# Routing done tile by tile between the output projection's matmuls, in a transformer block with 32 experts

## The reference

```
x += concat[GLA heads, stick-breaking heads] @ w_out
x += cross_attention(rmsnorm(x), rmsnorm(mem))          # ends with o @ w_mo
h  = rmsnorm(x, g_ffn)
logits = h @ w_router + b_router                        # 512 x 32
top_vals, top_idx = top_k(logits, 4)
gates = softmax(top_vals)
# pairs (token, expert) sorted by expert, in blocks of rows of one expert
for each block (rows xb, expert e):
    gu = xb @ w_gu[e] + b_gu[e]                         # 1024 -> 2048
    gate = min(gu[:, :1024], 7);  lin = clip(gu[:, 1024:], -7, 7)
    act = (lin + 1) * gate * sigmoid(1.702 * gate)
    y = act @ w_down[e] + b_down[e]                     # 1024 -> 1024
    x[token] += gates * y
y = rmsnorm(x, g_final)
```

## Time and profile before

| | us |
|---|---|
| median of 3 runs | 1733.54 (1732.9 to 1734.62) |
| the profiled execution | 1732.56 |
| its span, first to last instruction | 1730.7 |
| mean granted TensorE clock in it, as a share of full speed | 0.977 |
| busy in the span: PE / DVE / ACT / POOL | 1643.1 / 1075.6 / 831.3 / 133.2 |
| weights and data moved | 477.05 MB, 276 GB/s on average |

### The profile page before, as it was taken

The page is one execution under the profiler, slowest core; times in us unless marked ns, Lnnn a source line. Parts: engine busy times, 40 slices in busy tenths (PEclk is TensorE's granted clock), DMA queues, the critical chain, the costliest instruction groups (busy, mean ns, idle before and its releaser), DMA issues.

```text
span 1730.7 us, 26767 instructions
## 1 busy us (share of the span) xinstructions
PE 1643.1 (95%) x9998; PEld 1370.3 (79%) x9998; DVE 1075.6 (62%) x1139; ACT 831.3 (48%) x844; POOL 133.2 (8%) x216
## 2 busy tenths in 40 slices
PE   6999989999975999999999999999999999999995
PEld 5876657987744888888888888888888888888883
DVE  4221554434346677777777777777777777777774
ACT  4243364433321454555545555555555555555553
POOL 0020220000000000100001000010000100000000
PEclk9999989999987999999999999999999999999998
DMA  5111123422066899999999999999999999999993
GB/s 203 49 49 49 49 98 122 143 73 93 25 227 218 278 366 366 377 368 368 370 367 382 364 370 368 368 384 357 373 373 361 387 357 374 369 372 369 369 356 116
DMA packets 134772, 477.05 MB, mean 276 GB/s; under 512 B 10241, under 2 KB 10290, under 8 KB 134706
## 3 DMA queue, kind: packets, MB, share of 16 engines
q1 hardware_dynamic: 123968, 446.72, 69.1%
q0 software_dynamic: 7168, 25.17, 6.1%
q10 hardware_dynamic: 3602, 4.69, 0.9%
HBM read 457.67 MB, written 18.87 MB: 275 GB/s over the span
## 4 chain that ended last, share of the span: by engine, by line
PE 91%; DVE 4%; ACT 3%; issue 1%; DMA 1%; ACTq 0%; POOL 0%; DVEq 0%; POOLq 0%
PE psum L978 23%; PE psum L997 21%; PE psum L1022 21%; PE psum L610 17%; PE psum L789 1%; PE psum L778 1%; PE psum L972 1%; PE psum L964 1%; PE psum L766 1%; PE psum L881 1%; PE psum L901 1%; ACT ring_split L1116 1%; PE psum L915 0%; DVE ring_split L1509 0%; PE psum L889 0%
## 5 line engine op out<-in xcount | busy, mean ns | idle before, releaser
L978 PEld LDWEIGHTS psum<-MIX,ring 128*128 128x128 f32 x4096 | 775.7, 191 | 101.6 <-DVE MIX L1923 1.6
L978 PE MATMUL psum<-MIX,ring 128*128 128x96 f32 x4096 | 726.0, 260 | 1.1 <-DVE MIX L1923 1.1
L997 PE MATMUL psum<-ring_split,xs_hi 128*96 128x512 f32 x512 | 200.3, 437 | 0.0
L1884 DVE TENSOR_TENSOR ring_split<-ring,w_hi_a 128x2048 fp32r<-128x2048 f32 x64 | 146.3, 2288 | 84.2 <-ACT w_hi_a L1366 83.9
L1022 PE MATMUL psum<-ring_split,act_hi 128*96 128x512 f32 x512 | 198.1, 434 | 0.0
L1896 DVE TENSOR_TENSOR ring_split<-ring,w_hi_x 128x2048 fp32r<-128x2048 f32 x62 | 141.9, 2288 | 84.8 <-ACT w_hi_x L1377 84.8
L1884 DVE TENSOR_TENSOR ring_split<-ring,w_hi_x 128x2048 fp32r<-128x2048 f32 x64 | 146.4, 2289 | 72.2 <-ACT w_hi_x L1366 72.2
L610 PE MATMUL psum<-ring_split,H_hi 128*128 128x512 f32 (+1 forms) x512 | 151.2, 379 | 0.6 <-DVE ring L1595 0.6
L1896 DVE TENSOR_TENSOR ring_split<-ring,w_hi_a 128x2048 fp32r<-128x2048 f32 x62 | 141.6, 2284 | 2.5 <-ACT w_hi_a L1377 2.5
L1366 ACT ACTIVATE w_hi_a<-ring 128x2048 fp32r<-128x2048 f32 x62 | 117.7, 1898 | 12.3 <-DMA ring<-in_w_gu 12.3
L1366 ACT ACTIVATE w_hi_x<-ring 128x2048 fp32r<-128x2048 f32 x64 | 121.3, 1897 | 0.0
(11 more groups left out here) (290 smaller groups left out, 2656.8 us busy)
## 6 DMA issues: line engine op xcount, KB each, us to landing
ring<-in_w_gu SPq DMA_DIRECT2D x256, 1024.0 KB, 10.6
ring<-in_w_down SPq DMA_DIRECT2D x128, 1024.0 KB, 12.7
ring<-in_w_in SPq DMA_DIRECT2D x6, 2048.0 KB, 10.2
X<-in_x SPq DMA_DIRECT2D x8, 512.0 KB, 7.6
ring<-in_w_out SPq DMA_DIRECT2D x2, 2048.0 KB, 8.0
ring<-in_w_mk SPq DMA_DIRECT2D x2, 2048.0 KB, 8.9
ring<-in_w_mv SPq DMA_DIRECT2D x2, 2048.0 KB, 7.7
ring<-in_w_mq SPq DMA_DIRECT2D x2, 2048.0 KB, 8.5
```

What stands on the lines that cost most here:

```text
L978: return mm(psum[:, dst, q * C:(q + 1) * C], lhsT=gate_w(k // 2)[:, k % 2, f * P:(f + 1) * P], rhs=xsT[:, k, :], start=k == 0 and q == 0, ...
L997: x_last = mm(psum[0:C, L0 + half, :], lhsT=rows_, rhs=cols_, start=k == 0 and n == 0, stop=k == KT - 1 and n == 2, skip_group_check=True)
L1884: v.tensor_tensor(lin_lo(c), lin_w(c), chunk_hi(c).bitcast(F32), ALU.subtract)\
```

## The change

It makes three moves.

*Order.* `ROUTE` is a list of PE's steps. The parts of `y2` are kept, and between them stand, tile by tile, the transposes (`h3`), the logits (`lg`), the ranks (`rk`) and the products of the first-block table (`tb`). DVE and ACT get lists in the same order. The logits come out with tokens on partitions at once, so the transposes back go; the norm's gain is multiplied into the router's weights (`w_rt`), not into the rows, so the copies out of PSUM are plain; the bias is a row spread over partitions. The ranks of a tile are one product with the triangle, and one with ones on the running sum `picks_upto`.

*First-block table from ranks alone.* The item of a pick in the first block is its expert. The table of items 0 to 31 is the product of "slot equals rank" with the pick's one-hot over experts, with that one-hot times the row number, and with it times the gate. A rank of 96 or more matches no slot. The row number lacks the slot, and `table_out` subtracts it where the slot is taken. `s_first` then lets POOL gather.

*Overflow into item 0.* `overflow()` makes the number of items, the list of experts and the one-hots for items 32 to 52; PE adds their table up in 16 products behind the lin transposes of item 0; `overflow_out()` makes the integer tables and counts `s_items`. The engines read the number of items only behind that.

```
+ROUTE = [
+    ("y2", 0, 0), ("y2", 0, 1), ("y2", 1, 0), ("y2", 1, 1), ("h3", 0), ("y2", 2, 0), ("lg", 0), ("y2", 2, 1),
+    ("h3", 1), ("y2", 3, 0), ("h3", 2), ("lg", 1), ("rk", 0), ("y2", 3, 1), ("lg", 2), ("rk", 1), ("tb", 0),
+    ("h3", 3), ("rk", 2), ("lg", 3), ("tb", 1), ("tb", 2), ("rk", 3), ("tb", 3),
+]
...
 SP: the wait for s_items and the reads of n and m stand behind the loads of item 1's lin and gate
...
 PE
+            def route_logits(i):
+                b = begin(("lg", i))
...
+                    for k in range(4 * u, 4 * u + 4):
+                        last = mm(b[:, 0:E], lhsT=h3T[i % 2][:, k, :], rhs=w_rt[:, k, :], start=k == 0,
+                                  stop=k == KT - 1)
+            def route_ranks(i):
...
+                    mm(b[:, 0:E], lhsT=ones[:, :], rhs=picks_upto[:, i - 1, :], start=True, stop=False)
+                done(mm(b[:, 0:E], lhsT=before[:, :], rhs=picks[:, i, :], start=i == 0, stop=True))
+            def route_table(i):
...
+                for k in range(K):
+                    last = mm(b[0:C, 0:3 * E], lhsT=in_slot[i][:, k, :], rhs=pick_rhs[:, K * i + k, :],
+                              start=i == 0 and k == 0, stop=i == TT - 1 and k == K - 1)
...
-            pe.wait_ge(s_items, 1)
-            m = pe.value_load(last_item_i[0:1, 0:1], ...)
             item_transpose(0)
             lin_and_gate(0)
...
             lin_transpose(0)
+            pe.wait_ge(s_xnext, 2)
+            pe.wait_ge(s_over, 1)
+            for n in range(16):
+                last = mm(psum[0:C, Y0, 0:3 * MORE], lhsT=over_slot[:, n, :], rhs=over_rhs[:, n, :], ...)
+            last.then_inc(s_overt, 1)
             lin_and_gate(1)
+            pe.wait_ge(s_items, 1)
+            m = pe.value_load(last_item_i[0:1, 0:1], ...)
...
 ACT
+            norm(0); norm(1); h3_out(0); gate_exp(0); norm(2); h3_out(1); h3_out(2); gate_exp(1)
+            norm(3); h3_out(3); gate_exp(2); gate_exp(3)
...
 DVE (add = add_residual of y2)
+            add(0,0) add(0,1) add(1,0) add(1,1) h3_out(0) add(2,0) choose(0) add(2,1) h3_out(1) weigh(0)
+            sum_gates(0) add(3,0) h3_out(2) choose(1) rank(0) weigh(1) sum_gates(1) add(3,1) choose(2) rank(1)
+            h3_out(3) weigh(2) sum_gates(2) rank(2) choose(3) weigh(3) rank(3)
+            choose(i): logits + bias, max, max_index, neg, cast, onehot, picks, picks_upto, row one-hot
+            weigh(i): reciprocal, gates, gate one-hot      sum_gates(i): one sum
+            rank(i): onehot * ranks, sum, in_slot[i] = (slot == rank)
+            gate, dst = table_out(bank(("table",)), 0, E)          # four linked operations
+            dve.sem_inc(s_first, 1)
...
             lin_lo_part(0, 0)
-            lin_lo_part(0, 1)
             xT_next(0)
             xT_lo(0)
             xT_place(0)
+            lin_lo_part(0, 1)
             lin_lo_part(0, 2)
             lin_lo_part(0, 3)
+            overflow()
             xT_next(1, 6)
...
             a_lo(0, 0)
+            overflow_out()
             lin_lo_part(1, 2)
+            m = dve.value_load(last_item_i[0:1, 0:1], ...)
...
 POOL
-            pool.wait_ge(s_items, 1)
+            pool.wait_ge(s_first, 1)
             first_gather(0)
...
             scatter(1)
+            pool.wait_ge(s_items, 1)
+            n = pool.value_load(n_items_i[0:1, 0:1], ...)
```

## The result

The changed kernel takes 1720.88 us (median of 4 runs, 1719.63 to 1722.44) against 1733.7 for the kernel before (4 runs): ratio 0.9923, 95% interval 0.991 to 0.9935. That is 12.8 us faster. I had forecast 1711 us and a range of 1707 to 1719, so direction and place were right, and nearly half of the gain is missing. The profiled execution took 1721.68 us, its span is 1719.9.

What follows compares the result with a forecast made beforehand. PE bounds the steady loop (36.11 us a turn), so only the 55.2 us serial routing before the first expert product could shrink: 1732.56 - 20.7 - 1.7 + 0.2 + 0.3 = 1710.7, forecast 1711, range 1707 to 1719 us.

Steps and rivals of the forecast that it cites:

- t0: Start of the first expert product, forecast at E + 28.3 = 524.3 us, against 545.05 before.
- the stores cost 0.3: Item 0: lin remainders waiting through ACT for four accumulator stores were to cost 0.3 us, bounds 0 to 1.3.
- Step 1: Output projection: early tiles' transposes, logits and a rank product add 6.2 us of PE work, ending it at 496.0.
- Step 2: From projection end to first-block table: DVE's routing chain, PE's share beside it, table at E + 14.2.
- E: End of the output projection, forecast at 489.83 + 6.2 = 496.0 us.
- Step 3: From the table to the first expert product: gather and DVE strands, product at E + 28.3, gain 20.7 us.
- The bias products' first bank 1.1: DVE strand between table and first expert product: 1.1 us counted for the first bank of bias products.
- Step 4: Item 0: overflow takes 13.4 us in DVE's idle stretch, ends at t0 + 20.6, costs nothing; bound read 0.2, stores 0.3.
- Step 5: Clock around item 1's start: overflow products shorten PE's idle stretch, gaining 1.7 us (bounds 0 and 1.7).
- Rival 1: First gather and accumulator stores queue behind the weights: gather +9.5, stores 1.3, total 1722 us; chance 0.07.
- Rival 2: DVE late in item 0 (+2.2, overflow 17 us) or in the interleaved tiles (+4.5): 1717.5 us; chance 0.13.
- Rivals 3 and 4: Third: weights bound the loop, 1738.5 us, chance 0.03. Fourth: an early wait keeps routing serial, 1733 us, chance 0.03.

Runs made afterwards that it cites:

- e4: Changed kernel plus unread products filling PE's idle time before the first expert product and some behind the overflow products: 1719.18 us, ratio 0.9906.
- e13: Changed kernel with overflow() cut in two around lin remainders, plus unread products keeping PE busy up to the first expert product: 1718.86 us.
- e7: Changed kernel with item 0's gate chunks 2 and 3 and down loads held until the accumulator stores landed: 1722.93 us, ratio 0.9936.
- e6: Changed kernel with overflow() cut in two, its first half between lin remainders 1 and 2 of item 0: 1718.13 us, ratio 0.9908.
- e12: Changed kernel with item 0's lin weights loaded ahead of the row writes and overflow() cut in two: 1715.73 us.
- e15: Changed kernel unaltered, rerun as control on the chip of three other runs: 1722.76 us.

## Why the prediction was wrong, step by step

The mechanism of the gain was right: the routing did move between the projection's products and t0 came earlier. Three of my terms failed. I had "the stores cost 0.3" and item 0 costing nothing, and item 0 took 3.3 us more than that; I had PE's small products lying beside DVE at the full clock, and at the lower clock they put 3.9 us on the way to t0; and I counted 1.7 us of clock in item 1 as gained, and 2.7 less than that came.

**Step 1 held.** The projection ends at 496.39; I had 496.0. PE has no hole between its halves.

**Step 2 was short by 1.9 us**: table at E + 16.1, not 14.2. The count of DVE operations was right: with PE kept at full clock it stood at E + 14.05. I had priced PE's share as lying beside DVE. At the lower clock it does not: the fourth tile's logits took 3.56 us, 1.97 at the full clock, and DVE stood still 1.47 us for them and 0.62 for the ranks behind them.

**Step 3 was short by 2.0 more**: t0 at E + 32.24, not 28.3. "The bias products' first bank 1.1" was 2.16, since the 16 products took 4.92 us instead of 3.02; DVE's adds ended at E + 26.8, not 22.9, and set t0 (`[4.05 <-DVE X L1971]`). The gather was hidden, so its price did not matter here; the gathers of that line took 8.3 us in the middle, my 8.7. With PE kept at full clock (e4, e13) the gather ends last, as in my sum, and t0 is E + 28.2.

**Step 4 failed in one term, and in one that was not there.** `overflow` itself took 541.21 to 554.72 = 13.5 us (13.4 forecast). Wrong was "the stores cost 0.3": I let them land in 4.6, or 8.7 as a gather under load. They took up to 11.6 us. From 523 to the last landing they shared the engines with the weights. The page's queues in 523 to 526 (queue, packets, MB, share of the 16 engines), ACT's first, then SP's:
```profile
q10 hardware_dynamic: 169, 0.63, 51.2%
q1 hardware_dynamic: 163, 0.62, 50.7%
```
The four stores are 2.1 MB; at half of 416 GB/s that is 10.1 us, and from its first packet to the last landing the queue took 11.9 (522.9 to 534.8). In 529 to 532 a gather was the third with work, and the shares were 38.1% and 37.5%, and 27.1% for the gather. The Trainium skill, "DMA: Bandwidth & Descriptors" (queues, rings and completion order), says that each engine takes turns between the queues that have work, packet by packet; the trace agrees. I had used the rule to say that stores don't queue, and not to say at what rate they go. The rate is not all: the first store was issued at 518.92, and its queue moved nothing until 522.9, 4.0 us later. Before the change, with no weights in flight, it was 0.9 us (533.16 to 534.0). What holds the start back no run here shows. So `overflow` ended at t0 + 26.1 instead of 20.6, and item 1 was placed 3.8 us later after t0 than before (36.5 against 32.7). Missing altogether was the landing of item 1's lin weights. Before, they had come at t0 + 12.7 and 16.8; now the DMA engines are full till 561 and they come at t0 + 20.2 and 24.5. It costs little while DVE is late itself, and all of DVE's repair is lost on it (e7, e6). Both have to go for the 3.8 us to come back: e12 has t0 + 33.2.

**Step 5 failed.** The 1.7 us of clock did not come back, and 1.0 more went. PE did run the overflow products, but DVE came later than they ended: PE waited 4.18 and 0.86 us instead of 2.70 and 1.06, and the clock was 0.50 in 565 to 570. (My "PE stood still there" in step 4 had overlooked the product at 576.32.) The stretch from placing to outputs is 20.0 us, before the change 19.0. In e15, where PE waited 2.38 and 1.06, the clock was 0.80 in 565 to 570 and the stretch 19.1.

**The sum.** Against 1710.7: E +0.4, table +1.9, table to t0 +2.0, item 0 +3.3 (3.8 less my 0.5), clock +2.7, and the tail behind item 1's linear outputs +0.8 (1134.7 us against 1133.9): 11.1, where 1721.68 - 1710.7 = 11.0. The tail is spread between executions as far as it shows: in e15, the same kernel, it is 1133.9. The forecast's own range was narrower than its terms: all at their late end they add up to 7.6, which makes 1718, and I wrote 1716.

**The rivals.** Rival 1 named the stores' delay but took it at 1.3 us, and put 9.5 on the gather, which did not happen; its 1722 is near the result by coincidence. Rival 2's place, DVE behind in item 0, is where 3.3 us went, by another cause: `overflow` ran its 13.5 us, but started late. Rivals 3 and 4 are out: turns of 36.11, and the routing does interleave. My chances were fair on the sign and too narrow on the size: the sum had six terms that could only come later, and I let each be shielded by slack from a profile in which the DMA engines and PE's clock were in another state.

## What to carry to other kernels

A stage that moves earlier meets other traffic and another clock than the profile shows: price its transfers at the share of bandwidth they get beside what will then be in flight, and its small products at the lower clock. When an engine's step and a transfer end within a few us of each other, try the two edits together, since each alone may measure as nothing. Look for windows with few GB/s ahead of a stretch in which the DMA engines are full; a load behind an unrelated wait on the same queue is the first suspect. When one kernel's runs differ by more than the edit is worth, compare profiles with the same fall of the clock, from a mark in the program on.

## What was unexpected of the hardware

With PE busy for 4.1 of 5 us, in small products with idle gaps of 0.7 and 0.9 us ahead of the fall, the granted clock still fell, to 0.74 and 0.58 in the two windows from 500; with added products it stayed at 1.00. When it falls differs between executions of one program: the same 16 logits products took 3.56 and 1.94 us. The two profiles' spans are 3.7 us apart, for whatever else differs between them. The Trainium skill, "TensorE: Matmul & The Clock Gate" (part 1), says of the clock's rise at a kernel's start that its moment varies from run to run; these two profiles show the same of a fall in the middle of a kernel.

Two queues that both had work took 51.2% and 50.7% of the engines, and a queue whose transfer was issued while the engines were full of another's stood 4.0 us without moving anything, against 0.9 with the engines empty.
